# A two-block transformer kernel on one core: its first transfers, waits and lows in another order, and its inverse roots by another iteration

## What is computed

```python
def swiglu(h, w_in, w_out):
    a, b = jnp.split(h @ w_in, 2, axis=-1)
    return (jax.nn.silu(a) * b) @ w_out

for layer in range(2):
    h = h + 0.5 * swiglu(rmsnorm(h, ffn_norm[layer, 0]), ffn_w_in[layer, 0], ffn_w_out[layer, 0])
    hn = rmsnorm(h, mix_norm[layer])
    h = h + (mlstm_mixer(hn, ...) if layer == 0 else nsa_mixer(hn, kv, ...))
    h = h + 0.5 * swiglu(rmsnorm(h, ffn_norm[layer, 1]), ffn_w_in[layer, 1], ffn_w_out[layer, 1])
    if layer == 0:
        kv = nsa_shared_kv(h, kv_norm, kv_w, cmp_pe, cmp_w1, cmp_w2, k_norm)
for i in range(2):
    x = layer_norm(4 ** 0.25 * x + (fox_mixer, dsa_mixer)[i](x), ln_g[i], ln_b[i], 1e-5)

# in the mLSTM:  h_out = num / max(|den|, exp(-m));  (rmsnorm(h_out) * sigmoid(og)) @ w_out
# in dsa, for a block of 128 queries:
isc = relu(qi . ki) * wi summed over 8 index heads, causal
_, idx = lax.top_k(isc, 64)
p = softmax(q_full . kv_lat[idx]);  o = (p @ ckv[idx]) @ w_uv;  out = (silu(gate) * o) @ w_out
```

## Time and profile before

| | us |
|---|---|
| runs | 1385.69, 1385.78, 1382.89 |
| median | 1385.69 |
| the profiled execution | 1382.88 |
| its span, first to last instruction | 1381.2 |
| PE, PEld, DVE, ACT, POOL busy in it | 1302.3, 1099.3, 877.3, 616.9, 21.7 |
| mean granted clock of PE in it | 0.979 |

### The profile page before, as it was taken

The page is one execution under the profiler, slowest core; times in us unless marked ns, Lnnn a source line. Parts: engine busy times, 40 slices in busy tenths (PEclk is TensorE's granted clock), DMA queues, the critical chain, the costliest instruction groups (busy, mean ns, idle before and its releaser), DMA issues.

```text
span 1381.2 us, 16655 instructions
## 1 busy us (share of the span) xinstructions
PE 1302.3 (94%) x6797; PEld 1099.3 (80%) x6797; DVE 877.3 (64%) x1329; ACT 616.9 (45%) x836; POOL 21.7 (2%) x36
## 2 busy tenths in 40 slices
PE   5999999879999999999999988989999999989887
PEld 4888888778788888878888865878888999868765
DVE  5555557595655557685866587665555675577664
ACT  5444446434344445534444465534443354434531
POOL 1000000100000000000000000000000000000000
PEclk9999999999999999999999999999999999999899
DMA  8665545333555555547564230355556765246001
GB/s 277 222 193 190 184 155 191 112 126 124 178 193 190 193 190 170 173 155 235 183 213 159 104 110 1 122 166 194 191 192 131 184 193 175 63 152 244 32 0 61
DMA packets 158780, 218.18 MB, mean 158 GB/s; under 512 B 8224, under 2 KB 110960, under 8 KB 158704
## 3 DMA queue, kind: packets, MB, share of 16 engines
q1 hardware_dynamic: 156848, 212.56, 47.8%
q0 software_dynamic: 1376, 3.71, 0.9%
q10 hardware_dynamic: 480, 0.85, 0.2%
...
## 4 chain that ended last, share of the span: by engine, by line
PE 82%; DVE 12%; ACT 3%; issue 2%; DMA 1%; ACTq 0%; POOL 0%; DVEq 0%
PE PS L658 23%; PE PS L659 22%; PE PS L661 22%; DVE wlo L1987 3%; PE PS L775 1%; PE PS L689 1%; PE PS L690 1%; ACT whi L1472 1%; PE PS L678 1%; PE PS L974 1%; DVE XL L2026 1%; ACT XH L1494 1%; PE PS L696 1%; PE PS L1258 1%; PE PS L1244 1%
## 5 line engine op out<-in xcount | busy, mean ns | idle before, releaser
L1987 DVE TENSOR_TENSOR wlo<-raw,whi 128x2048 fp32r<-128x2048 f32 (+3 forms) x207 | 459.4, 2230 | 125.1 <-ACT whi L1472 124.4
L1472 ACT ACTIVATE whi<-raw 128x2048 fp32r<-128x2048 f32 (+3 forms) x207 | 383.0, 1865 | 60.9 <-DMA raw<-in_fox_w_in_dram 33.5
L658 PE MATMUL PS<-whi,XL 128*128 128x512 f32 (+3 forms) x992 | 389.0, 393 | 21.6 <-DVE scr L2088 7.5
L659 PE MATMUL PS<-wlo,XH 128*128 128x512 f32 (+3 forms) x992 | 382.0, 386 | 0.0
L661 PE MATMUL PS<-whi,XH 128*128 128x512 f32 (+3 forms) x992 | 265.2, 384 | 0.0
L658 PEld LDWEIGHTS PS<-whi,XL 128*128 128x128 f32 x992 | 188.7, 190 | 58.6 <-DVE scr L2088 8.6
L659 PEld LDWEIGHTS PS<-wlo,XH 128*128 128x128 f32 x992 | 188.8, 190 | 33.2
L661 PEld LDWEIGHTS PS<-whi,XH 128*128 128x128 f32 x992 | 185.8, 190 | 35.8
L1526 ACT ACTIVATE scr<-PS,rn 128x256 f32<-128x256 f32 x88 | 41.7, 474 | 226.7 <-PE PS L661 224.0
L658 PE MATMUL PS<-whi,GL 128*128 128x512 f32 x320 | 125.4, 392 | 0.0
L659 PE MATMUL PS<-wlo,GH 128*128 128x512 f32 x320 | 124.6, 389 | 0.0
...
## 6 DMA issues: line engine op xcount, KB each, us to landing
raw<-in_ffn_w_in_dram SPq DMA_DIRECT2D x176, 512.0 KB, 4.8
raw<-in_ffn_w_out_dram SPq DMA_DIRECT2D x88, 512.0 KB, 4.9
raw<-in_fox_w_in_dram SPq DMA_DIRECT2D x24, 512.0 KB, 7.8
raw<-in_a_w_in_dram SPq DMA_DIRECT2D x16, 512.0 KB, 4.4
raw<-in_dsa_w_in_dram SPq DMA_DIRECT2D x16, 512.0 KB, 5.6
raw<-in_kv_w_dram SPq DMA_DIRECT2D x12, 512.0 KB, 4.1
...
raw<-in_a_w_out_dram SPq DMA_DIRECT2D x8, 512.0 KB, 4.8
```

The costliest lines, as they stand in the source:

```text
L658: mm(o, xl, wh, start=start and i == 0, stop=False, skip_group_check=True)
L659: mm(o, xh, wl, start=False, stop=False, skip_group_check=True)
L1472: A(whi[:, p % SLOTS, 0:n], raw[:, p % SLOTS, 0:n], ACT.Copy).then_inc(hi_done, 1)
L1987: V.tensor_tensor(wlo[:, p % SLOTS, 0:n], raw[:, p % SLOTS, 0:n], whi[:, p % SLOTS, 0:n].bitcast(F32), ALU.subtract).then_inc(lo_done, 1)
```

## The change

Its parts, in the order of the program:

- **First transfers.** Half 0 of x goes first on SP's queue, half 1 third on ACT's. Piece 0 is loaded by four DMAs: k 0 and 1 (`lead_in`), k 2 and 3 (`landed[0]`); its high and low are made in two halves of 128x1024 each (`lead_hi`, `lead_lo`, then `hi_done`, `lo_done`), and PE's first products wait for the first half only. An activation of one column `warm` with Sigmoid stands ahead of the first XH.
- **First mixer.** The gate columns go ahead of two lows and a copy on DVE; an activation of one column with Sigmoid stands behind the Exp of `m_floor`. PE waits for each piece of a chunk and not for the last one only (also in kv, nsa, fox and dsa). `turn_heads(1)` moves behind the products of tile 0 with the first two of the four output pieces.
- **Feed-forwards 1 to 3.** The second low of the first step is made behind silu(1, 0) and not before silu(0, 0).
- **Roots.** The guess has another constant, the first step fitted factors, and the second and last is of third order: ten operations for twelve. There are 16 such roots in the program.
- **Last mixer.** The copy `d_krT` stands ahead of the low of piece 9 (of the stage), the low of piece 11 ahead of `mask_four` 0, half of `choose(1)`'s rounds between `mask_four` 0 and 1, and `low_of_z` 0 ahead of `mask_four` 3.

Tile 1's eight transposes and their wait have moved behind tile 0's first output products. The diff, without the declarations of semaphores and of `warm`:

```diff
--- before.py
+++ after.py
@@ -32,6 +32,10 @@
 ALPHA = (2 * 2) ** 0.25
+ROOT_A = 0.703952253
+ROOT_L = (3 / (8 * ROOT_A ** 2)) ** (1 / 7)
+ROOT_C = 2.38924456 * ROOT_A * ROOT_L
+ROOT_B = ROOT_A * ROOT_L ** 3
@@ -532,7 +541,7 @@
         def _(sp):
-            sp.dma_start(h[:, 1, :], a["x"][0, P:T, :]).then_inc(x_in[1], 16)
+            sp.dma_start(h[:, 0, :], a["x"][0, 0:P, :]).then_inc(x_in[0], 16)
@@ -560,6 +569,11 @@
                         dst = raw[:, p % SLOTS, :].rearrange("p (k w n) -> p k w n", k=4, w=2)
+                        if p == 0:
+                            for part, there in ((slice(0, 2), lead_in), (slice(2, 4), landed[0])):
+                                for w in range(2):
+                                    sp.dma_start(dst[:, part, w, :], w_in[:, part, w, 0:FC]).then_inc(there, 16)
+                            continue
@@ -681,10 +695,14 @@
                 for i, (w, ks) in enumerate(banks):
-                    if los[i]:
+                    if los[i] == 1:
+                        pe.wait_ge(lead_lo, 1)
+                    elif los[i]:
...
                     for j, (k, wh, wl) in enumerate(ks):
+                        if los[i] == 1 and j == 2:
+                            pe.wait_ge(lo_done, 1)
@@ -826,7 +843,7 @@
                         o = PS[:, b0 + t, 0:n]
-                        first_products(o, stage, t, banks)
+                        first_products(o, stage, t, banks, (0, 0) if t else (end, 0) if whole else (end - 1, end))
@@ -840,6 +857,8 @@
                     for i, (p, kn) in enumerate(ps):
+                        if m == 0:
+                            pe.wait_ge(lo_done, p + 1)
@@ -1078,9 +1097,8 @@
             og_products(6, 1, 3)
-            for t in range(NT):
-                turn_heads(t)
-            out_stage("mlstm_out")
+            turn_heads(0)
+            out_stage("mlstm_out", lambda: turn_heads(1))
@@ -1167,14 +1185,12 @@
                 o = PS[:, n_bank(t, c), 0:n]
-                if t == 0:
-                    pe.wait_ge(lo_done, end)
...
                         banks.append((w, [(4 * w + k, wh[:, k, :], wl[:, k, :]) for k in range(4)]))
-                    first_products(o, "nsa", t, banks)
+                    first_products(o, "nsa", t, banks, (0, 0) if t else (end - 1, end))
@@ -1182,6 +1198,8 @@
                     for i, (p, kn) in enumerate(ps):
+                        if t == 0:
+                            pe.wait_ge(lo_done, p + 1)
@@ -1357,12 +1375,12 @@
                     n, end = stages["dsa"][1][c][2], chunk_end("dsa", c)
-                    if t == 0:
-                        pe.wait_ge(lo_done, end)
...
                                 turn_h("dsa", 1, w)
+                        if t == 0:
+                            pe.wait_ge(lo_done, end - 1 + i)
@@ -1590,11 +1608,17 @@
                 .then_inc(par_in, 16)
-            act.dma_start(h[:, 0, :], a["x"][0, 0:P, :]).then_inc(x_in[0], 16)
+            act.dma_start(h[:, 1, :], a["x"][0, P:T, :]).then_inc(x_in[1], 16)
             act.dma_start(con[:, C_CAUS:C_ALL], a["con"][:, C_CAUS:C_ALL]).then_inc(con_in, 16)
+            act.wait_ge(warm_set, 1)
+            A(warm[:, :], warm[:, :], ACT.Sigmoid)
...
             x_hi("ffn0", 0)
-            split_to(1)
+            act.wait_ge(lead_in, 32)
+            A(whi[:, 0, 0:PIECE // 2], raw[:, 0, 0:PIECE // 2], ACT.Copy).then_inc(lead_hi, 1)
+            act.wait_ge(landed[0], 32)
+            A(whi[:, 0, PIECE // 2:PIECE], raw[:, 0, PIECE // 2:PIECE], ACT.Copy).then_inc(hi_done, 1)
+            split[0] = 1
@@ -1634,6 +1658,7 @@
             A(m_floor, o[:, 0:16].rearrange("p (t h) -> p t h", t=NT), ACT.Exp, scale=-1.0).then_inc(side_act, 1)
+            A(warm[:, :], zcol, ACT.Sigmoid)
@@ -1997,15 +2022,16 @@
                 link(V.tensor_scalar(y.bitcast(U32), v.bitcast(U32), 1, None, ALU.logical_shift_right))
-                V.tensor_scalar(v, v, -0.5, None, ALU.mult).then_inc(dve_step, 1)
+                V.tensor_scalar(v, v, -ROOT_A * ROOT_L, None, ALU.mult).then_inc(dve_step, 1)
                 steps[0] += 1
-                link(V.tensor_scalar(y.bitcast(I32), y.bitcast(I32), -1.0, float(0x5F3759DF), ALU.mult, ALU.add))
-                for i in range(3):
-                    link(V.tensor_tensor(t_, y, y, ALU.mult))
-                    link(V.tensor_tensor(t_, t_, v, ALU.mult))
-                    if i < 2:
-                        link(V.scalar_tensor_tensor(out=y, in0=t_, scalar=1.5, in1=y, op0=ALU.add, op1=ALU.mult))
-                V.scalar_tensor_tensor(out=to[:, 0:w], in0=t_, scalar=1.5, in1=y, op0=ALU.add, op1=ALU.mult)\
+                link(V.tensor_scalar(y.bitcast(I32), y.bitcast(I32), -1.0, float(0x5F1FFFF9), ALU.mult, ALU.add))
+                link(V.tensor_tensor(t_, y, y, ALU.mult))
+                link(V.tensor_tensor(t_, t_, v, ALU.mult))
+                link(V.scalar_tensor_tensor(out=y, in0=t_, scalar=ROOT_C, in1=y, op0=ALU.add, op1=ALU.mult))
+                link(V.tensor_tensor(t_, y, y, ALU.mult))
+                link(V.tensor_tensor(v, t_, v, ALU.mult))
+                link(V.scalar_tensor_tensor(out=t_, in0=v, scalar=10 * ROOT_B / 3, in1=v, op0=ALU.add, op1=ALU.mult))
+                V.scalar_tensor_tensor(out=to[:, 0:w], in0=t_, scalar=5 * ROOT_B * ROOT_B, in1=y, op0=ALU.add, op1=ALU.mult)\
@@ -2096,12 +2122,14 @@
                     p = p0 + in_piece(f, i)
-                    split_to(p + AHEAD + 1)
+                    late = 1 if f and i == 0 else 0
+                    split_to(p + AHEAD + 1 - late)
...
                         during(i, 0)
+                    split_to(p + AHEAD + 2 - late)
+                    silu(1, i)
                     split_to(p + AHEAD + 2)
-                    silu(1, i)
@@ -2187,12 +2215,16 @@
+            V.memset(warm[:, :], 0.0).then_inc(warm_set, 1)
...
                 x_lo("ffn0", 0, w)
-            split_to(1)
+            for part, there, out in ((slice(0, PIECE // 2), lead_hi, lead_lo), (slice(PIECE // 2, PIECE), hi_done, lo_done)):
+                dve.wait_ge(there, 1)
+                V.tensor_tensor(wlo[:, 0, part], raw[:, 0, part], whi[:, 0, part].bitcast(F32), ALU.subtract).then_inc(out, 1)
+            split[0] = 1
@@ -2261,12 +2293,12 @@
             values_in(2)
-            o = odd_bank("mlstm", 3)
-            V.tensor_copy(m_qT[:, 2:4, :], two(o)).then_inc(chunk_dve, 1)
...
             dve.wait_ge(side_dve, looks(side_no["m_a"], "dve"))
+            o = odd_bank("mlstm", 3)
+            V.tensor_copy(m_qT[:, 2:4, :], two(o)).then_inc(chunk_dve, 1)
@@ -2718,11 +2750,12 @@
             dve.wait_ge(side_src, src_no["ki_ckv"])
-            split_to(first + 10)
+            split_to(first + 9)
...
             V.tensor_copy(d_krT[0:32, :], o[0:32, 0:T]).then_inc(side_dve, 1)
+            split_to(first + 10)
@@ -2741,16 +2774,19 @@
-            def choose(t):
+            def choose(t, rounds=range(8)):
...
                 cm = caus[:, P:2 * P] if t == 0 else caus
-                link(V.tensor_tensor(work, isc, cm, ALU.subtract))
-                for _ in range(8):
+                if 0 in rounds:
+                    link(V.tensor_tensor(work, isc, cm, ALU.subtract))
+                for _ in rounds:
...
                     link(V.match_replace(work, d_m8[:, :], work, -3e38))
+                if 7 not in rounds:
+                    return
@@ -2778,12 +2814,13 @@
+            split_to(first + 12)
             mask_four("dsa", 0, d_mask)
+            choose(1, range(4))
             mask_four("dsa", 1, d_mask)
-            split_to(first + 12)
...
             scale_four("dsa", 1)
-            choose(1)
+            choose(1, range(4, 8))
@@ -2791,8 +2828,8 @@
             split_to(first + 14)
+            low_of_z("dsa", 0, z_mix)
             mask_four("dsa", 3, d_mask)
-            low_of_z("dsa", 0, z_mix)
```

6 lines of the change are left out of this document (5 added, 1 removed).

## The result

The changed kernel took 1355.13 us (median of 4 runs, 1350.23 to 1358.16), the kernel before 1385.74 (4 runs, 1382.89 to 1388.08). The two medians are 30.6 us apart (0.978 of before); the ratio on record is 0.976, with a 95% interval from 0.973 to 0.979. A gain of 34.9 us had been worked out from rows, and 1349.5 us forecast; the median lies inside the range of 1342 to 1362. The profiled execution took 1352.9, its span 1351.2, its mean granted clock 0.984 (before: 1381.2 and 0.979).

The account below looks back on a forecast made before the run. PE was taken as the bound, busy 1302.3 of 1381.2 us, its waits also slowing the clock. Terms summed to 34.9 us: 1348.0 from the profiled execution, 1350.8 from the median, so 1349.5; range 1342 to 1362.

Parts of the forecast that it names:

- Gate columns: First mixer: moving two short DVE operations earlier removes PE's wait before L1015; 7.4 us, or 4.2 without the clock.
- two feed-forwards: Starts of ffn1 and ffn3: a later low and shorter root cut PE's wait for the silu; 4.3 us each (2.6).
- chunk 2: Last mixer: with a wait per piece, the first half runs during the 5.73 us wait; 5.3 us (4.0 if slow).
- chunk 5: Last mixer: a low moved ahead of eight masked rows removes a 3.32 us wait; 4.0 us (3.3 to 4.7).
- The start: First transfers and products: earlier x and split piece 0, then piece 1 gates the second half; 2.5 us (0.5 to 3.9).
- fourth rival: At the start: the swap of x's halves brings nothing, costing 1.5 us, total about 1351 us; chance 0.15.
- The output: Last mixer's output: a low moved ahead of four masked rows cuts a 2.69 us wait; 1.8 us (1.0 to 2.5).
- Roots: Two fewer chained operations save 0.4 us where a root gates PE; elsewhere two in sparse mixer, one in last norm, 1.2.
- Added waits: 26 new PE waits on lows of pieces done long before, taken to cost 0 us.
- third rival: Slower: each of 26 added waits stops PE's queue; at 1.5 us each, about 1389 us; chance 0.03.
- first rival: The clock stays low: only idle time is gained, 22 to 26 us, giving about 1361 us; chance 0.22.
- second rival: DVE becomes the bound: lows come late downstream, some 10 us of the gain goes, about 1358 us; chance 0.15.

Follow-up runs that it names:

- e5: The changed kernel run again with no edit: mean 1354.8 us over six runs, ratio to the kernel before 0.976.
- e1: The changed kernel with the old root of twelve chained operations put back: mean 1359.9 us over four runs.
- e4: The changed kernel with the low of the last mixer's third output piece put behind DVE's two copies of transposed weights: mean 1351.0 us over five runs.
- e11: The changed kernel with the two halves of x back in their old queues and places: mean 1357.3 us over six runs.
- e3: The changed kernel with the low of z of tile 0 put back behind the fourth group of masks: mean 1354.4 us over four runs.
- e2: The changed kernel with PE again waiting once per chunk, for its last piece's low, in all mixers: mean 1361.8 us over four runs.
- e6: The kernel before with only the gate columns moved ahead of two lows and a copy on DVE: mean 1383.7 us over ten runs, ratio 0.998.
- e10: The changed kernel with eight unread 128x512 products between the scores of the last mixer's first two groups: mean 1351.7 us over six runs.

## Why the prediction came out as it did

- **The sum of edges** was right as a method and nearly so in its size: 34.9 forecast, 30.0 between the two traces, 32.5 between the means of 23 and 6 runs. The idle part is where it was put: PE's idle time fell by 25.6 us (24 forecast). The clock part is not: PE's busy time fell by 3.4 (0.4 in e5) and not by 8 to 12.
- **Gate columns** 7.4 for 7.4, **heads** 4.5 for 4.1, **two feed-forwards** 4.0 each for 4.3, **chunk 2** 5.6 for 5.3, **chunk 5** 4.9 for 4.0, **index** 0.0 for 0, in the pair of traces. Their waits went as worked out; that the clock's parts came too is partly luck of the execution. At the gate columns the stretch is back in e1 and e4, which takes 3 of the 7.4; at chunk 5 it is 10.2 us long in e5 where it was 6.8, which takes 1.0. In chunk 2 the clock stayed at 1.00 though PE waited 1.67 in it, which the low end of that term had doubted.
- **The start** gave 3.6 for 2.5. Piece 1 was the gate, as said (its high began at 13.6, its low ended at 17.8). Most of the difference is that it landed some 0.8 us earlier than the 14.4 reckoned, so that the second half came 4.5 and not 3.7 earlier; of the 1.2 deducted for a lower clock behind it 0.9 came. The fourth rival, the swap that brings nothing, fell by e11, in which the second half of the products came 1.7 later; its price (1.5) was right.
- **The output** is the step that failed: 1.8 forecast, 0.1 found, and e3 shows that the move of the low of z is worth nothing by itself. The prediction saw that transposes would be next and late by 1 to 2 us; it did not count the low of piece 14 that stands between masks and copy, and which made it 3.06. e4 takes this low away and gains 3.8.
- **Roots**: the sum was right (0.4 at each of ffn1 and ffn3 and in chunk 2, and 1.2 elsewhere, 2.4 in all), the places were not. e1 shows the 0.4 also at ffn2, where the sum had nothing, and at the gate columns; in the sparse mixer it is there once and not twice, in chunk 2 not at all.
- **Added waits**: free, as forecast; e2 bounds some twenty of them to 0.3 us in all. The third rival wanted 1.35 for each.
- **The clock.** Here the mechanism was wrong and the size too large. The forecast took each slow stretch as the consequence of one long wait, to be gained with it, and put 8 to 12 us on it. In the pair of traces slow work of PE fell by only 7.4 us, worth 3.7, since stretches stood at new places (-0.8, -1.4, -3.2, and behind the 3.06); over the runs it was some 7 by the estimate under e5. More idle time and tail than forecast (27 for 24) made up for part of it. One row spoke against it beforehand. The prediction says of all four stretches of the earlier trace rows that PE had stood idle for 2.7 us or more before them or at their start; the longest began at 1298.4, after PE had been busy at full clock since 1294.3, and its wait of 3.32 came only at 1302.8:

```profile
1294.30:1298.30 4.00, 4.00 (x20) 2.88 (x20) 1.58 (x6) 0.30 (x1) 0.00 (x0) 1.00 0.01 2
1298.40:1302.80 4.40, 4.40 (x13) 2.98 (x12) 0.20 (x2) 1.25 (x8) 0.00 (x0) 0.50 0.00 0
```

e4 against e5 shows a stretch come and go over identical instructions, e6 one behind a wait of 0.7, e10 one that follows the work and not a wait. The first rival, that the stretches follow something else, is therefore true in part, and its sign, a busy time as before, is there in e5 (1301.9 for 1302.3). Its number (1361) is too high: the mean clock did rise with the change, from 0.9734 to 0.9823. Which of the edges raised it is not shown.
- **The level.** The profiled execution of before (1382.88 at 0.979) was one of its faster ones; 23 runs have a mean of 1387.4. Taking half-way between it and the median of three runs put the forecast some 3 us low. Together with the 2.4 us in the gain this is all of the 5.3 between 1349.5 and the mean of 1354.8.
- DVE as the next bound (second rival) did not come: in the last mixer the waits on `wlo` are 1.7 us in all, for 9.1. The one new long wait on DVE is the 3.06 at the output. (Its price was put some 1.5 us low: ten less than the forecast of 1349.5 is 1359.5 and not 1358.)
